# Leaving out the one-column product with the identity in front of each series of 64x64 products

## The reference

```python
def step(state, inp):
    r_t, w_t, k_t, v_t, a_t, b_t = inp
    sa = jnp.einsum('bhvk,bhk->bhv', state, a_t)
    state = state * w_t[:, :, None, :] + sa[..., None] * b_t[:, :, None, :] + v_t[..., None] * k_t[:, :, None, :]
    return state, jnp.einsum('bhvk,bhk->bhv', state, r_t)
```

## Time and profile before

| what | value |
|---|---|
| median of 3 runs | 2968.7 us (2968.13 to 2971.97) |
| the profiled execution, its own time | 2963.58 us |
| its span, first to last instruction | 2961.5 us |
| TensorE busy | 2879.3 us (97%) |
| DVE busy, ACT busy | 833.1 us (28%), 362.7 us (12%) |
| the stretch of the change | 96.9 to 180.6 us of the span |

### The profile page before, as it was taken

One profiled execution on the slowest core, in us unless ns is written; L12 is line 12 of the kernel. 1 busy time (PEld: TensorE's weight loads), 2 busy tenths in 40 slices (PEclk: granted clock), 3 DMA queues, 4 the chain that ended last, 5 costly groups with the idle time before them and its releaser, 6 DMA issues.

```text
span 2961.5 us, 35466 instructions
## 1 busy us (share of the span) xinstructions
PE 2879.3 (97%) x14699; PEld 1892.5 (64%) x14700; DVE 833.1 (28%) x1902; ACT 362.7 (12%) x738; POOL 28.6 (1%) x56
## 2 busy tenths in 40 slices
PE   8999999989999999999999999999999999998999
PEld 7967778833333333333337888777788888876888
DVE  2546441222222222222223111642211121035110
ACT  2122320200000000000002000122100000013000
POOL 0000000000000000000000000000000000000000
PEclk9999999999999999999999999999999999999999
DMA  5122234559999999999995434322343333332430
GB/s 204 58 97 93 100 136 154 199 232 420 429 428 429 428 428 429 428 428 428 428 429 204 148 140 164 114 97 82 108 147 141 145 133 146 140 143 75 153 142 15
DMA packets 50090, 654.91 MB, mean 221 GB/s; under 512 B 6016, under 2 KB 8208, under 8 KB 10912
## 3 DMA queue, kind: packets, MB, share of 16 engines
q1 hardware_dynamic: 45696, 642.90, 54.1%
q0 software_dynamic: 3136, 9.38, 1.0%
q10 hardware_dynamic: 1152, 1.05, 0.1%
HBM read 652.26 MB, written 1.05 MB: 221 GB/s over the span
## 4 chain that ended last, share of the span: by engine, by line
PE 85%; DMA 8%; DVE 4%; ACT 1%; issue 1%; PEldq 0%; PEld 0%; SPq 0%; DVEq 0%; ACTq 0%
PE bank L314 73%; DMA weight_ring<-weight_stream 8%; PE bank L1113 2%; PE bank L2124 1%; PE bank L2093 1%; DVE expert_hidden L2226 1%; DVE expert_hidden L2225 1%; PE bank L2115 1%; PE bank L1366 0%; ACT expert_y_slots L2171 0%; PE bank L737 0%; PE bank L3051 0%; PE bank L747 0%; PE bank L3030 0%; PE bank L1119 0%
## 5 line engine op out<-in xcount | busy, mean ns | idle before, releaser
L314 PE MATMUL bank<-ffn_x_gained,weight_ring 128*128 128x272 f32 (+1 forms) x2816 | 637.7, 389 | 3.7 <-DVE ffn_x_gained L2399 2.1
L314 PEld LDWEIGHTS bank<-ffn_x_gained,weight_ring 128*128 128x128 f32 x2816 | 534.1, 190 | 107.0 <-DVE ffn_x_gained L2399 3.4
L314 PE MATMUL bank<-weight_ring,expert_x_slots_t 128*64 128x512 f32 x2048 | 460.8, 601 | 4.0 <-DMA weight_ring<-weight_stream 4.0
L314 PEld LDWEIGHTS bank<-weight_ring,expert_x_slots_t 128*64 128x64 f32 x2048 | 141.4, 138 | 320.6 <-issue 305.8
L314 PE MATMUL bank<-x,first_weight_ring 128*128 128x256 f32 x1376 | 316.6, 386 | 15.9 <-DMA first_weight_ring<-weight_stream 8.2
L314 PE MATMUL bank<-ffn_h,weight_ring 128*128 128x272 f32 (+1 forms) x1408 | 319.0, 389 | 2.1 <-DVE ffn_up L2497 2.1
L314 PEld LDWEIGHTS bank<-ffn_h,weight_ring 128*128 128x128 f32 x1408 | 267.2, 190 | 54.0 <-DVE ffn_up L2497 3.8
L314 PEld LDWEIGHTS bank<-x,first_weight_ring 128*128 128x128 f32 x1376 | 261.7, 193 | 58.7 <-issue 18.9
L314 PE MATMUL bank<-weight_ring,expert_hidden_slots_t 128*64 128x512 f32 x1024 | 225.2, 592 | 0.0
L314 PEld LDWEIGHTS bank<-weight_ring,expert_hidden_slots_t 128*64 128x64 f32 x1024 | 73.4, 137 | 146.4 <-issue 123.2
L2235 DVE TENSOR_TENSOR moe_rows<-moe_rows,bank 128x512 f32<-128x512 f32 x128 | 79.4, 683 | 269.1 <-PE bank L2124 269.1
(11 more groups left out here) (607 smaller groups left out, 2153.9 us busy)
## 6 DMA issues: line engine op xcount, KB each, us to landing
weight_ring<-weight_stream SPq DMA_DIRECT2D x276, 2048.0 KB, 15.4
first_weight_ring<-weight_stream SPq DMA_DIRECT2D x29, 2048.0 KB, 7.7
first_weight_ring<-weight_stream SPq DMA_DIRECT2D x4, 512.0 KB, 12.2
x<-x_t SPq DMA_DIRECT2D x2, 512.0 KB, 7.3
out_t<-x ACTq DMA_DIRECT2D x8, 128.0 KB, 1.9
c_ret_ret_q<-const_ret_q POOLq DMA_DIRECT2D x1, 544.0 KB, 5.1
c_ret_ret_k<-const_ret_k POOLq DMA_DIRECT2D x1, 544.0 KB, 5.8
c_odd_pool_inv<-const_pool_inv POOLq DMA_DIRECT2D x1, 544.0 KB, 3.8
```

What stands on the lines that cost most here:

```text
L314: ins = K.nc.tensor.matmul(out, lhsT, rhs, start=start, stop=stop)
```

## The change

The function `gate` and its 10 calls in the code (56 products when it runs) are taken out. The waits stay where they are, now directly in front of the first product of the series. No other line changes.

```diff
-    def gate(b):
-        nc.tensor.matmul(bank[b][0:32, 511:512], eye[:, 0:32], eye[:, 0:1], start=True, stop=True)
...
                 if i >= 2:
                     pe.wait_ge(*kept.take())
-                gate(b + half)
                 for n in units(half):
                     ins = product(into(b + half, n), of(x, n), of(o, n))
                 ins.then_inc(*made.post())
...
                 if i:
                     pe.wait_ge(*turned_sb.take())
-                gate(4 + half)
...
             for half in range(2):
-                gate(4 + half)
                 for n in units(half):
                     ins = product(into(4 + half, n), at_unit(ak, n), at_unit(rows_v, n))
...
                 pe.wait_ge(*joined_sb.take(2))
-                gate(half)
...
                 pe.wait_ge(*joined_sb.take())
-                gate(2 + half)
...
                 pe.wait_ge(*s_sb.take())
-                gate(0)
...
             if c < NCH - 1:
-                gate(4)
...
             if c:
                 pe.wait_ge(*w_sb.take())
-            gate(1)
...
             if c >= 2:
                 pe.wait_ge(*y_sb.take())
-            gate(2 + c % 2)
...
             pe.wait_ge(*u_sb.take())
-            gate(0)
```

## The result

The changed kernel took 2947.86 us (median of 3 runs, 2945.07 to 2950.59), against 2968.7 us before: 20.8 us less, a ratio of 0.9933 with a 95% interval of 0.9910 to 0.9956. Two later series of the same two kernels, with more runs, gave 0.9945 (0.9926 to 0.9965) and 0.9954 (0.9940 to 0.9968), or 13.1 and 14.1 us between the medians. What follows is first where the time went, then why the first comparison showed more.

A forecast was written before the change was run, and what follows sets the result against it. TensorE was taken to bound the kernel up to the experts, where the weight stream sets the pace. 15.4 us for gates less 0.4 and 0.27 us of waits gave 14.7 us, 2968.7 to 2954.0 us; range 2949.3 to 2961.

The forecast's parts named there:

- The price of a gate: Branch on TensorE: a gate with 64x64 products on both sides costs 0.30 us, beside other work 0.15 us.
- two changes of shape: At each gate: 0.15 us for the tile shape change before it and 0.15 us for the one behind.
- The three kinds of gates: 47 between 64x64 series, 14.1 us; 5 behind 128x128 products, 0.75 us; 4 behind an exposed wait, 0.6 us.
- each part: Net saving by consecutive parts of the branch: A 5.2 us, B (the levels) 5.4 us, C (the chunks) 4.1 us.
- The new waits: Waits exposed without gates: 0.08 us in each of five levels of B, 0.4 us, and 0.27 us in C.
- the one in the first chunk: C's first chunk: B needs ACT's copy of U and waits 0.27 us; in later chunks it stays hidden.
- A's masks and ACT's copies: Part A: DVE masks at 0.69 us per series of 0.93, ACT's copies every two series; nothing new exposed.
- The three rivals: Chain's figure is the whole cost (0.07), a satisfied wait costs as much as the gate (0.08), granted clock falls (0.03).
- a satisfied wait costs nothing: Against the rival that a satisfied wait costs a boundary 0.30 us, leaving 4.7 us won, 2964.0 us; chance 0.08.
- the change of shape went with the gate: Against the rival that it stays at each boundary, a gate worth 0.15 us, 8.6 us in all, 2960.1 us; chance 0.07.
- the clock was 1.00 over the stretch: Against the rival that 64x64 products fall to 1.2 GHz without gates, 54 us more, 3008 us; chance 0.03.
- SP's waits: 90 to 600 us, for line 314: 463.8 us; the weight stream follows TensorE, so a gain in the branch stays.

The follow-up runs named there:

- the four shapes: Kernel before with each gate kept but reshaped: 64x64 on one half, stretch 75.4 us; 64x64 on each half, 76.0; 64x32, 83.8; 128x64, 87.0.

## Why the prediction was right, and where it went wrong

- **The price of a gate** (0.30 us between 64x64 products, 0.15 beside other work) was right, and in the main its reading as two changes of shape too: the doubled gate and the four shapes show it. It left out the product itself, which by the doubled gate may have 0.06 of the 0.30 us. The distance of two ungated series in the earlier trace rows was the row that carried it.
- **The three kinds of gates and the sum**: 15.4 us less the stalls. The stretch lost 14.78 us against 14.7, each part within 0.15 us, so the sum isn't right by errors that cancel.
- **The new waits**: 0.08 us in each level came out as forecast, before S3 in the first and before S2 in the others; the one in the first chunk was 0.18 instead of 0.27, because ACT now starts 0.68 us behind U instead of 0.73, where U's first product stood behind a gate, and TensorE starts 0.06 us behind ACT. A's masks and ACT's copies stayed hidden.
- **The three rivals** fell in one view: part A runs at 0.94 us a series through 11 satisfied waits, so a satisfied wait costs nothing; the change of shape went with the gate; the clock was 1.00 over the stretch (the last column but two):

```profile
96.43:165.83 69.40, 65.92 (x1893) 61.91 (x1893) 34.43 (x53) 9.01 (x19) 0.00 (x0) 1.00 0.02 6
```

- **The gain stays.** From the end of the branch to the same record near the end of the expert stage both kernels take nearly the same time at the same DMA share, 1359.43 us before and 1358.83 after:

```profile
181.09:1540.52 1359.43, 1323.50 (x6038) 632.15 (x6038) 415.70 (x898) 180.45 (x296) 9.51 (x18) 0.99 0.79 330
```

```profile
165.83:1524.66 1358.83, 1323.14 (x6038) 632.21 (x6039) 415.75 (x898) 180.25 (x296) 9.51 (x18) 0.99 0.79 330
```

  So the saturated DMA stretch begins and ends earlier with the branch, as argued from SP's waits.
- **The step that failed** is the last one: "I put the same saving on the median", with "3 us for the spread". What failed is the base that the saving was put on and the allowance for the spread, not the cost of the gates. The median of 3 runs before, 2968.7, was itself high: later sets of the same kernel gave 2963.52, 2964.93 and 2967.05, and the three runs of the changed kernel came out low, 2947.86 against 2950.43 and 2950.85 later. The gap of 5.1 us between the profiled execution and the median stood in the prediction and was carried over instead of being asked about. By the profiled execution (2963.58 - 14.7 = 2948.9) the median would have been met within 1.1 us, in part by luck, since the later medians of the changed kernel lie 1.5 and 2.0 us above that. The four executions that the prediction names already span 8.4 us, from 2963.58 to 2971.97, where it allowed 3. In the first 29 later executions of the kernel before the spread is 15 us, from 2960 to 2975, and it goes with the granted clock: the mean falls from 0.991 to 0.986. Since the lower level is half of the upper, 0.005 of the mean is 0.010 of 2961 us spent there, 30 us, in which at most half, 15 us, is lost (an estimate). The range should have allowed for that on either median.

What stays open is whether the form of the code moves the places where the low clock is granted. In the twelve traces it comes up at the same few places, near 126, 440 and 475 us behind the end of the branch for instance. A place at 41 us has it in nine of them; the changed kernel shows it in its second and third profile and not in the first, so that place is not the kernel's doing. But a place at 396 to 399 us has it (10.2 us each) only with the gate doubled, on both halves or in the shape 64x32. These three took 446.7, 446.7 and 443.5 us from line 314 behind the branch to the experts' first product, where the kernel before and the first profile of the changed one take 436.3 (617.42 - 181.09 and 602.16 - 165.83) and the other executions up to 441.7. They are single executions, and the kernel before has executions with a mean clock of 0.986 of its own. It wasn't tried with more runs.

## What to carry to other kernels

Where small products run in tiles of the array, count the changes of tile shape on TensorE, not the products: a cheap product in another shape costs 0.30 us, as much as five of the small ones (ten records of 0.029 us). The price is found by comparing two neighbouring series with and without such a boundary, not by the duration of the odd instruction. And before a saving of half a per cent is put on a median of three, look at how far the profiled execution lies from it, and at how long either had the lower clock level. Stretches of two kernels are best cut at the same record, not at the same distance in time.

## What the runs showed of the hardware

- One product of one column in another tile shape costs 0.30 us between streams of 64x64 float32 products, with 128x32 and with 64x32; a second one behind it 0.06, so the change of shape and back is about 0.24. With 128x64 it is 0.35, of which 0.21 instead of 0.15 us lie between the gate's start and the next product.
- In the shape of the stream a record of one column takes 0.029 us, as long as one of 64 columns, if the products alternate between the halves (1.05 against 0.93 us a series for four more records). A product on half 0 alone, in front of another on half 0, costs 0.12 us.
- A satisfied semaphore wait in front of a product costs nothing that shows in a spacing of 0.93 us.
- The lower clock level came up in all twelve traces at the same few places, for longer or shorter, 50.6 to 98.8 us in all. One kernel's time differs by 15 us in 2960 between executions, and goes with the mean granted clock.
